# Both MLP products of a two-layer transformer kernel by one level of Strassen's algorithm

## The reference, cut to what matters

```python
def sqrelu_mlp(x, w_up, w_down):
    return jnp.square(jax.nn.relu(x @ w_up)) @ w_down
...
        x = layer_norm(ALPHA * x + mix, ln_gain[layer, 0], ln_bias[layer, 0])
        x = layer_norm(ALPHA * x + sqrelu_mlp(x, mlp_w_up[layer], mlp_w_down[layer]), ln_gain[layer, 1], ln_bias[layer, 1])
```

## Time and profile before

| | us |
|---|---|
| median of 3 runs | 1406.59 |
| lowest, highest | 1405.65, 1408.8 |
| span of the profiled execution | 1407.9 |
| TensorE busy in it | 1389.6 |
| VectorE, ScalarE, GpSimd busy | 468.9, 196.1, 80.0 |

### The profile page before, as it was taken

One profiled execution on the slowest core, in us unless ns is written; L12 is line 12 of the kernel. 1 busy time (PEld: TensorE's weight loads), 2 busy tenths in 40 slices (PEclk: granted clock), 3 DMA queues, 4 the chain that ended last, 5 costly groups with the idle time before them and its releaser, 6 DMA issues.

```text
span 1407.9 us, 17372 instructions
## 1 busy us (share of the span) xinstructions
PE 1389.6 (99%) x6758; PEld 853.1 (61%) x6758; DVE 468.9 (33%) x1064; ACT 196.1 (14%) x493; POOL 80.0 (6%) x110
## 2 busy tenths in 40 slices
PE   9999999999999999999999999999999999999996
PEld 8677585675756876775765867754444444444433
DVE  1236442422460364522416444522122222221223
ACT  2135200000002251000001232300000000000001
POOL 1016300000000001000000010000000000000001
PEclk9998999999999999999999999999999999999999
DMA  9921164544444316756651533189999999999994
GB/s 382 357 79 57 61 257 191 179 181 172 183 164 165 127 57 237 269 190 236 259 210 63 223 120 147 63 336 420 421 421 421 415 421 420 421 422 420 421 421 204
DMA packets 51002, 359.47 MB, mean 255 GB/s; under 512 B 5888, under 2 KB 6096, under 8 KB 8432
## 3 DMA queue, kind: packets, MB, share of 16 engines
q1 hardware_dynamic: 45248, 324.60, 57.7%
q0 software_dynamic: 5392, 32.05, 6.4%
q10 hardware_dynamic: 288, 1.80, 0.3%
HBM read 356.88 MB, written 1.05 MB: 254 GB/s over the span
## 4 chain that ended last, share of the span: by engine, by line
PE 88%; DVE 2%; issue 0%; ACT 0%; ACTq 0%; DVEq 0%
PE ps L910 16%; PE ps L892 14%; PE ps L1330 13%; PE ps L1359 7%; PE ps L1255 6%; PE ps L1308 6%; PE ps L848 6%; PE ps L738 4%; PE ps L809 2%; PE ps L743 2%; PE ps L782 2%; PE ps L871 1%; PE ps L797 1%; PE ps L701 1%; PE ps L1078 1%; PE ps L1215 1%
## 5 line engine op out<-in xcount | busy, mean ns | idle before, releaser
L910 PE MATMUL ps<-ring,qk_tiles 128*128 128x512 f32 x512 | 221.4, 592 | 0.0
L892 PE MATMUL ps<-xT,ring 128*128 128x256 f32 x896 | 194.7, 379 | 0.0
L892 PEld LDWEIGHTS ps<-xT,ring 128*128 128x128 f32 x896 | 170.1, 190 | 25.6 <-issue 2.9
L910 PEld LDWEIGHTS ps<-ring,qk_tiles 128*128 128x128 f32 x512 | 97.1, 190 | 118.1 <-issue 117.7
L738 PE MATMUL ps<-xT,ring 128*128 128x256 f32 x432 | 94.6, 379 | 0.8 <-DVE xT L1824 0.8
L1308 PE MATMUL ps<-masked_and_probs,probT 128*128 128x512 f32 x208 | 94.4, 594 | 1.0 <-DVE masked_and_probs L2407 1.0
L1255 PE MATMUL ps<-masked_and_probs,mix_rows 128*128 128x256 f32 (+1 forms) x416 | 93.0, 376 | 0.0
L1255 PEld LDWEIGHTS ps<-masked_and_probs,mix_rows 128*128 128x128 f32 x416 | 75.0, 190 | 28.8 <-issue 19.6
L738 PEld LDWEIGHTS ps<-xT,ring 128*128 128x128 f32 x432 | 81.5, 190 | 11.9 <-ACT xT L1463 1.0
L2407 DVE TENSOR_TENSOR masked_and_probs<-ps,gate_rows 128x512 f32<-128x512 f32 x52 | 33.5, 686 | 152.4 <-PE ps L1359 152.4
L848 PE MATMUL ps<-ring,xT 128*128 128x512 f32 x192 | 84.0, 593 | 0.0
(11 more groups left out here) (433 smaller groups left out, 1820.9 us busy)
## 6 DMA issues: line engine op xcount, KB each, us to landing
ring<-in_stream SPq DMA_DIRECT2D x200, 1024.0 KB, 8.6
qk_tiles<-in_stream SPq DMA_DIRECT2D x46, 1024.0 KB, 19.8
qk_tiles<-in_ada POOLq DMA_DIRECT2D x12, 1024.0 KB, 6.0
vec_rows<-in_stream SPq DMA_DIRECT2D x12, 1024.0 KB, 17.0
con<-in_stream SPq DMA_DIRECT2D x12, 1024.0 KB, 18.6
y_rows<-in_stream SPq DMA_DIRECT2D x12, 1024.0 KB, 20.1
par<-in_stream SPq DMA_DIRECT2D x12, 1024.0 KB, 20.6
xT<-in_stream SPq DMA_DIRECT2D x11, 1024.0 KB, 22.1
```

The source lines that it names most:

```text
L892: mm = pe.matmul(ps[:, bank, (m % 2) * T:(m % 2 + 1) * T], w[:, kk, m * P:(m + 1) * P], xT[:, k, :], start=bank not in started, stop=k == ...
L910: mm = pe.matmul(ps[:, q, :], hT[:, k, t * P:(t + 1) * P], ws[k // 2][:, k % 2, half * 512:(half + 1) * 512], start=k == 0, stop=k == 7)
```

## The change

Each product of a step is cut into 2 x 2 blocks (token halves of 128, inner halves of 512, column halves of 512) and made of seven block products in Winograd's form instead of eight, which needs sums of blocks.

- TensorE: seven up products U1 to U7 of 16 matmuls with 128 moving columns (`up_product`), and seven down products D1 to D7 of four matmuls with 512 moving columns (`down_product`). Several accumulate in one PSUM bank, and each now has waits of its own ahead of it.
- GpSimd makes three weight combinations for the up product (`up_differences`, for the next step) and three for the down product (`down_differences`), each as two tensor-tensor operations of 1024 elements per partition whose two inputs both lie in SBUF: twelve a step. They share GpSimd's queue with the modulation loads. The first group of a layer stands in `start_mlp`, during the attention's output product.
- VectorE makes the fourth weight combination of each product (one operation of 2048 and two of 1024 elements), the four sums of token blocks (once a layer for the up product, in every step for the down product, `half_sums`), takes four hidden quarters (an add with one PSUM input, then ReLU and square in one operation, `hidden`), and makes eight additions to `y` instead of four (`add`). Its 16 modulation operations stay, in other places.
- ScalarE copies four partial products out of PSUM.
- The `w_up` chunks arrive in another order (`UP_ORDER`), and all modulation weights go through two slots.

The diff, cut to its core:

```diff
+UP_ORDER = (0, 2, 3, 1, 4, 5, 6, 7)
+
+
 def streamed(n):
 
+    for name in ("mlp0", "mlp1"):
+        step, at = divmod(n - FIRST[name], RING)
+        if 0 <= step < MLP_STEPS:
+            return n - at + UP_ORDER[at]
...
+        block4 = lambda w: w.rearrange("p (k n) -> p k n", k=4)
+        halves = gaterow[:].rearrange("p t f -> p (t f)")
+        halves = [block4(halves[:, 512 * i:512 * (i + 1)]) for i in range(4)] + [block4(probT[:, i, :]) for i in range(2)]
+
+        x_sums = [halves[0], halves[1], halves[2], quarters(xT, 1, 0)]
+        h_sums = [halves[4], halves[5], halves[3], quarters(hT, 1, 0)]
+
+        up_second, up_third = block4(mix[:].rearrange("p t f -> p (t f)")), block4(qk[:, 16:24, :].rearrange("p a b -> p (a b)"))
+
+        rows2 = lambda w: w.rearrange("p (k n) -> p k n", k=2)
+        down_second, down_third = [rows2(x[:, i, :]) for i in range(2)], [rows2(vec[:, 2 * i, :]) for i in range(2)]
...
+                def up_product(weights, tokens, bank, fresh=False, within=None):
+
+                    for m in range(4):
+                        if within and m == 2:
+                            within()
+                        for kk in range(4):
+                            mm = pe.matmul(ps[:, bank, m * P:(m + 1) * P], weights[:, kk, m * P:(m + 1) * P], tokens[:, kk, :],
+                                           start=fresh and m == 0 and kk == 0, stop=kk == 3, skip_group_check=True)
+                    return mm
+
+                def down_product(hidden, weights, bank, fresh=False, within=None):
+
+                    for kk in range(4):
+                        if within and kk == 2:
+                            within()
+                        mm = pe.matmul(ps[:, bank, :], hidden[:, kk, :], weights[kk // 2][:, kk % 2, :],
+                                       start=fresh and kk == 0, stop=kk == 3, skip_group_check=True)
+                    return mm
...
+                def up(it, first):
+                    b11, b12, b21, b22 = up_blocks(n0)
+                    if first:
+                        wait_columns(name, 0)
+                    chunk(n0, 1, it)
+                    up_product(b11, quarters(xT, 0, 0), 4, True).then_inc(s_prod, 1)
+                    chunk(n0 + 3, 1, it)
+                    up_product(b21, quarters(xT, 0, 1), 5, True, (lambda: turn_rows(x, name, 1)) if first else None).then_inc(s_prod, 1)
+
+                    pe.wait_ge(s_diff, it * 6 + (6 * done + 3))
+                    if first:
+                        pe.wait_ge(s_half, HALF_SUMS * layer + 1)
+                    up_product(b12, x_sums[0], 6, True).then_inc(s_used, 2)
+
+                    pe.wait_ge(s_taken, it * 4 + (4 * done + 1))
+                    if first:
+                        pe.wait_ge(s_half, HALF_SUMS * layer + 2)
+                    up_product(up_second, x_sums[1], 4).then_inc(s_prod, 1)
+
+                    pe.wait_ge(s_taken, it * 4 + (4 * done + 2))
+                    if first:
+                        pe.wait_ge(s_half, HALF_SUMS * layer + 3)
+                    chunk(n0 + 2, 1, it)
+                    up_product(b22, x_sums[2], 6).then_inc(s_used, 1)
+
+                    pe.wait_ge(s_taken, it * 4 + (4 * done + 3))
+                    if first:
+                        pe.wait_ge(s_half, HALF_SUMS * layer + 4)
+                    up_product(up_third, x_sums[3], 4).then_inc(s_prod, 1)
+
+                    pe.wait_ge(s_last, it * 2 + (2 * done + 1))
...
+                def down(it, last):
+                    b11, b12, b21, b22 = down_blocks(n0)
+                    for i in (4, 5):
+                        chunk(n0 + i, 1, it)
+                    pe.wait_ge(s_h, it * 8 + (8 * done + 2))
+                    down_product(quarters(hT, 0, 0), b11, 0, True).then_inc(s_prod, 1)
+                    for i in (6, 7):
+                        chunk(n0 + i, 1, it)
+                    pe.wait_ge(s_h, it * 8 + (8 * done + 4))
+                    down_product(quarters(hT, 0, 1), b21, 2, True).then_inc(s_prod, 1)
+
+                    pe.wait_ge(s_diff, it * 6 + (6 * done + 6))
+                    pe.wait_ge(s_half, it * 4 + (HALF_SUMS * layer + 6))
+                    down_product(h_sums[0], b12, 1, True).then_inc(s_used, 2)
+                    if last and hook:
+                        hook()
+
+                    pe.wait_ge(s_half, it * 4 + (HALF_SUMS * layer + 7))
+                    pe.wait_ge(s_y, it * 8 + (8 * done + 1))
+                    down_product(h_sums[1], down_second, 0).then_inc(s_prod, 1)
+
+                    pe.wait_ge(s_half, it * 4 + (HALF_SUMS * layer + 8))
+                    pe.wait_ge(s_y, it * 8 + (8 * done + 3))
+                    down_product(h_sums[2], b22, 1).then_inc(s_prod, 1)
+
+                    pe.wait_ge(s_half, it * 4 + (HALF_SUMS * layer + 9))
+                    pe.wait_ge(s_y, it * 8 + (8 * done + 4))
+                    down_product(h_sums[3], down_third, 0).then_inc(s_prod, 1)
+
+                    pe.wait_ge(s_last, it * 2 + (2 * done + 2))
+                    down_product(quarters(hT, 1, 1), b21, 3, True, before_last if last else None).then_inc(s_used, 2)
+
+                up(0, True)
+                down(0, False)
                 with pe.Fori(1, MLP_STEPS - 1) as it:
-                    step(it, False)
-                step(MLP_STEPS - 1, True)
...
+                    take(4, 0, 0)
+                    act.wait_ge(s_used, it * RING + (n0 + 2))
+                    take(6, 1, 1)
+                    act.wait_ge(s_prod, it * 9 + (9 * done + 3))
+                    take(4, 0, 1)
+                    act.wait_ge(s_prod, it * 9 + (9 * done + 4))
+                    take(4, 1, 0)
 
...
+            def half_sums(rows, outs, it, before):
+
+                q11, q12, q21, q22 = (quarters(rows, t, half) for t in range(TT) for half in range(2))
+                dve.tensor_tensor(outs[0], q21, q22, ALU.add).then_inc(s_half, 1)
+                dve.wait_ge(s_half, it * 4 + (before + 1))
+                dve.tensor_tensor(outs[1], outs[0], q11, ALU.subtract).then_inc(s_half, 1)
+                dve.wait_ge(s_half, it * 4 + (before + 2))
+                dve.tensor_tensor(outs[2], q12, outs[1], ALU.subtract).then_inc(s_half, 1)
...
+                    at = quarters(hT, t, half)
+                    dve.tensor_tensor(at, at, block4(ps[:, bank, :]), op).then_inc(s_h, 1)
+                    dve.wait_ge(s_h, it * 8 + (8 * done + 2 * n - 1))
+                    dve.scalar_tensor_tensor(out=at, in0=at, scalar=0.0, in1=at, op0=ALU.max, op1=ALU.mult).then_inc(s_h, 1)
...
+                def add(t, half, bank, op=ALU.add):
+
+                    at = y[:, t, half * 512:(half + 1) * 512]
+                    dve.tensor_tensor(at, at, ps[:, bank, :], op).then_inc(s_y, 1)
...
+                    dve.wait_ge(s_taken, it * 4 + (4 * done + 1))
+                    dve.wait_ge(s_prod, it * 9 + (9 * done + 2))
+                    hidden(it, 1, 0, 0, 5, ALU.add)
+                    dve.wait_ge(s_diff, it * 6 + (6 * done + 3))
+                    b21 = up_blocks(n0)[2]
+                    dve.tensor_tensor(b21, up_second, b21, ALU.subtract).then_inc(s_last, 1)
+                    modulate(layer, it, 0)
+                    modulate(layer, it, 1)
+                    dve.wait_ge(s_taken, it * 4 + (4 * done + 3))
+                    dve.wait_ge(s_used, it * RING + (n0 + 3))
+                    hidden(it, 2, 0, 1, 6, ALU.add)
+                    dve.wait_ge(s_taken, it * 4 + (4 * done + 4))
+                    hidden(it, 3, 1, 1, 4, ALU.add)
+                    dve.wait_ge(s_used, it * RING + (n0 + 4))
+                    hidden(it, 4, 1, 0, 7, ALU.subtract)
+                    dve.wait_ge(s_h, it * 8 + (8 * done + 8))
+                    half_sums(hT, h_sums, it, HALF_SUMS * layer + 5)
...
+                    dve.wait_ge(s_prod, it * 9 + (9 * done + 5))
+                    add(0, 0, 0)
+                    dve.wait_ge(s_prod, it * 9 + (9 * done + 6))
+                    added(it, 1)
+                    add(0, 0, 2)
+                    if last:
+                        added(it, 2)
+                        half_stats(0)
+                    dve.wait_ge(s_diff, it * 6 + (6 * done + 6))
+                    b21 = down_blocks(n0)[2]
+                    for i in range(2):
+                        w = dve.tensor_tensor(b21[i], down_second[i], b21[i], ALU.subtract)
...
+                        hook()
+                    modulate(layer, it, 2)
+                    dve.wait_ge(s_prod, it * 9 + (9 * done + 7))
+                    add(0, 1, 0)
+                    modulate(layer, it, 3)
+                    dve.wait_ge(s_prod, it * 9 + (9 * done + 8))
+                    added(it, 4)
+                    add(0, 1, 1)
+                    if last:
+                        added(it, 5)
+                        half_stats(1)
+                        norm(0)
+                    dve.wait_ge(s_prod, it * 9 + (9 * done + 9))
```

(58 more changed lines are left out.)

245 lines of the change are left out of this document (93 added, 152 removed).

## The result

The changed kernel takes 1509.2 us (median of 4 runs, 1506.9 to 1510.7) beside 1407.7 us for the kernel before (4 runs, 1405.7 to 1410.1): ratio 1.072, 95% interval 1.069 to 1.074. The forecast was 1476 us, the range 1404 to 1518: the sign and the range hold, the middle is 33 us short.

A forecast was written before the change was run, and what follows sets the result against it. TensorE's streaming bounds the MLP; products save 6 us a step, but VectorE and GpSimd excluding each other add more: 31 us a layer (62) plus 7 in the output products, 69 over 1406.6, gives 1476 us, range 1404 to 1518.

The forecast's parts named there:

- TensorE's part: MLP products: up 3.58 us, down 3.43, a step 49.1 instead of 55.1 us, 48 us saved over eight steps.
- The lengths beside it: Work added beside TensorE per MLP step: VectorE 31 us; GpSimd twelve operations of 2.36 us, 28.3; each would fit alone.
- the output product's wait in layer 0: Attention's output product: the norm on VectorE meets three GpSimd operations and TensorE waits 3.3 us.
- The walk's waits: TensorE's waits traced through MLP steps as VectorE and GpSimd exclude each other: 15.1 us in a middle step, making 64.2.
- The third rival: The clock falls too: half speed behind waits in the MLP, up to 2.5 us twice a step, 1490 to 1516 us; 22%.
- the forecast without it: The main case, waits from exclusion without any clock drop: 1476 us; 48%.
- its second bullet: Middle MLP step: six `up_differences` delay VectorE 11.8 us by turns; D3 waits 5.3 us, D4 3.8, D5 and D6 0.7.
- layer 1's first step: Second MLP's opening step: layer 1 taken as built the same as layer 0, whose first step is 68.5 us.
- the two output products: Attention's output products in both layers: TensorE waits 3.3 us for the norm, 7 us in both.
- Nothing is held up: Faster rival: the VectorE and GpSimd overlap does not exclude, so the MLPs gain: 1361 us; 16%.
- its walk of 200.0 us: MLP of one layer in the faster rival: steps of 50.4, 49.1, 49.1 and 51.4 us, 23 less than before.
- VectorE keeps the path: Rival: GpSimd gets in only in VectorE's longer pauses; step 53.7 us, kernel 1404 to 1412 us; 12%.

The follow-up runs named there:

- n5: Changed kernel with the relu and square of the hidden quarters moved from VectorE to ScalarE: 1480.8 us, ratio 1.053 to the kernel before.
- n9: Changed kernel with all GpSimd weight combinations moved to VectorE and each layer's first step reordered, relu and square on VectorE: 1368.0 us, ratio 0.973.
- n7: Changed kernel with GpSimd's issue of one modulation transfer moved behind the up part's six combinations, so they begin earlier: 1478.0 us, ratio 1.049.
- n2: Changed kernel with GpSimd waiting for its own semaphore after each of a step's twelve combinations: 1477.9 us, ratio 1.051.
- n11: Changed kernel with one GpSimd wait on itself per step, behind the first of the up part's six combinations: 1482.0 us, ratio 1.053.
- n1: Changed kernel with GpSimd's combinations cut to 16 elements per partition, so values are wrong: 1610.2 us with more expert work; a middle MLP step 49.05 us.

## Why the forecast was right in sign and 33 us short

**TensorE's part** was right to a tenth at full clock: up products of 3.58 us, down products of 3.43 to 3.44, a step without waits of 49.05 for a forecast 49.1.

**The lengths beside it** were right: VectorE 29.9 us a step where nothing holds it (forecast 31), GpSimd's operation 2.32 us (forecast 2.36), the output product's wait in layer 0 3.19 (forecast 3.3, by a norm operation that meets the end of the run). The Trainium skill's exclusion (SBUF — State Buffer, "Who interferes with whom") is what the traces show, n5 most plainly: 0.65 us for an addition with a PSUM input beside a busy GpSimd, 9.69 for one with two SBUF inputs.

**Where the missing time is.** The forecast was 69 us over the profiled execution of before, and the profiled execution of the changed kernel is 98.6 over it, 29.6 more (the other 4 us are the distances from span to median). The walk's waits add up to some 118 us, and TensorE's idle time rose by 117. The whole 29.6 us lie in its busy time: forecast 48 less, measured 18.4 less. For the MLPs alone it is busy for 422.5 us, where n9 does the same products in 400.7. So the term that was mis-sized is TensorE's busy time behind a wait, which the sum took at full clock.

**The third rival came true, then.** It had 22%, and the forecast without it 48%. After 16.36 us of idle TensorE the granted clock is at 0.50 (the lower of the two levels, 1.2 GHz) from 302 to 306 us and back at 1.00 from 307 on: D2 runs in 5.95 us instead of 3.60. Over the whole step the row is (columns as above):

```profile
257.07:324.99 67.92, 51.56 (x282) 36.43 (x280) 55.61 (x39) 2.39 (x4) 32.72 (x14) 0.87 0.42 155
```

16.36 of waiting and 2.35 of half clock make 18.7 of the 18.9 us over 49.05. The other four held steps pay 2.5 to 3.0 us behind D2, step 0 of layer 0 1.9 us each at D2 and D4, and the output products 1.8 us each behind their wait, close to the rival's 2.5. The time of 1509 lies inside its band of 1490 to 1516, by its own mechanism, though mostly with one long wait in a step where it had two short ones.

**The step of the walk that failed is its second bullet:** "GpSimd goes straight on to six `up_differences` at 30.8. They delay VectorE by four times 2.2 and twice 1.5". It took from the earlier trace rows that the path changes hands in each gap, and did not ask what happens where GpSimd leaves none. The run came when only one VectorE operation stood waiting, and it waited for all six: 16.36 us at D2 instead of 5.3, then nothing at D3 and D4 instead of 5.3 and 3.8. Of the six steps with an up part five went so, and in one the engines took turns. That a middle step's waits still add up to 16.4 us for a forecast 15.1 is luck. The page of n7, in which all six take turns, shows what they come to without the hold:

```profile
PE 1380.8 (94%) x7334; PEld 853.9 (58%) x7334; DVE 741.3 (50%) x1208; ACT 197.4 (13%) x493; POOL 346.7 (23%) x206
```

Of its span of 1476.8 us TensorE is idle for 96.0, so the hold costs 39 us of waiting and gives 10 back in busy time (more, shorter waits bring more half clock), 29.7 in all; n2 and n11 agree from another side.

**So the forecast's 1476 is n7's time for two wrong reasons that cancel.** n7 waits for 78 us more than the kernel before, 40 less than the walk's 118, and is busy for 39 more than the sum had. Its middle step from 254.52 to 317.45 is 62.93 us, forecast 64.2. But its waits are 3.83, 1.59, 3.00 and about 0.2, 8.6 us, not 15.1; the other 5 us are the half clock of D2 and D4 (6.67 and 5.40 us). The waits were oversized: a modulation that meets GpSimd takes 2.73 us, a delay of 1.98 and not 2.2, over twelve operations 2.6 us, and the later additions and sums had more room than the walk gave them.

**Two smaller terms.** The forecast took layer 1's first step for a copy of layer 0's (68.5 us); it is 77.3. Behind the norm VectorE's queue has the scaling of `qk_tiles` there, as in the kernel before, where nothing waited for what follows; now the half sums stand behind it and TensorE's third up product waits for them, 4.59 us, and runs at the lower clock (6.51 instead of 3.74). It waits as long in n1, so GpSimd has no part in it:

```profile
615.80 1.54 DVE L2373 TENSOR_SCALAR qk_tiles<-qk_tiles,small 128x1024 f32<-128x1024 f32 x2
617.54 0.69 DVE L2143 TENSOR_TENSOR gate_rows<-xT 128x512 f32<-128x512 f32 x1 [0.20 <-DVE qk_tiles L2373]
618.38 6.51 PE L897 MATMUL ps<-gate_rows,ring 128*128 128x128 f32 x32 [4.59 <-DVE gate_rows L2143]
```

And the two output products cost 5.1 and 6.1 us, not 7 together (1.6 of the 6.7 us up to the first up product were lost before its output product began): the wait of layer 1 is 4.17 us, not 3.3, and half clock follows both.

**The other rivals.** "Nothing is held up" has the right times for a kernel in which nothing is (layer 0 takes 199.8 us in n1 and 199.7 in n9), and its walk of 200.0 us is the best number of the prediction, though layer 1 takes 7 to 8 us more for the reason above; it was the wrong case only because GpSimd's work was there. "VectorE keeps the path" is the reverse of what the trace shows: it is GpSimd that can keep it.

## What to carry to other kernels

Work moved to GpSimd is not free because GpSimd is idle: count the VectorE operations with two SBUF inputs that run beside it, and look at how many GpSimd operations follow each other without a wait, since one run may hold VectorE for its whole length. If it must be there, put a wait for the operation just issued behind it (a wait that is already met left no gap here). Better, put the work on the engine that it would hold up, in an order that follows the products: here 14 us a step on VectorE cost nothing in the loop, where 28 us a step on GpSimd cost 13 to 19. The change itself, seven products for eight, is worth 40 us (2.7 to 2.9%) in that form. And where a forecast has TensorE wait, price the slower product behind the wait too: in the changed kernel the down product behind a wait of 5 or 16 us took 1.9 to 3.0 us longer than at full clock.
